# Convolution stage: the moving averages and some low halves go from VectorE to GpSimd, and VectorE's convolution taps move up

## The reference, cut to what matters

```python
def window_mean_minus_self(u, w):        # u: (1, 512, 128) of one group, w in (2, 4, 8, 16)
    cs = cumsum(u, axis=1)
    cs_lag = pad(cs, w)[:, :512]
    cnt = minimum(arange(512) + 1, w)
    return (cs - cs_lag) / cnt - u

def pool_conv_mixer(h, w_in, pool_w, pool_scale, dw_w, dw_b, ln_g, ln_b, w_out):
    u, glu_a, glu_b = split(h @ w_in, [512, 1024])
    pooled = stack([window_mean_minus_self(u[:, :, i], w) for i, w in enumerate((2, 4, 8, 16))])
    ya = einsum("btgc,gcd->btgd", pooled, pool_w) * pool_scale
    gl = glu_a * sigmoid(glu_b)
    cv = causal_dwconv(gl, dw_w) + dw_b      # 31 taps, 512 channels
    yb = silu(layernorm(cv, ln_g, ln_b))
    return concatenate([ya, yb]) @ w_out

# later, in each of two layers: cross attention to 256 memory rows, k, v = split(rmsnorm(mem) @ wkv, 2)
```

## Time and profile before

| What | us |
|---|---|
| Three timed runs | 1711.53, 1709.86, 1711.26; median 1711.26 |
| Profiled execution, first to last instruction (its span; no other time of it is given) | 1710.9 |
| TensorE busy in it | 1684.1 (98%) |
| VectorE busy in it | 1064.3 (62%) |
| GpSimd busy in it | 23.8 (1%) |

### The profile page before, as it was taken

One profiled execution on the slowest core, in us unless ns is written; L12 is line 12 of the kernel. 1 busy time (PEld: TensorE's weight loads), 2 busy tenths in 40 slices (PEclk: granted clock), 3 DMA queues, 4 the chain that ended last, 5 costly groups with the idle time before them and its releaser, 6 DMA issues.

```text
span 1710.9 us, 21153 instructions
## 1 busy us (share of the span) xinstructions
PE 1684.1 (98%) x8045; PEld 1374.0 (80%) x8045; DVE 1064.3 (62%) x1513; ACT 706.7 (41%) x1138; POOL 23.8 (1%) x42
## 2 busy tenths in 40 slices
PE   8999999999999999999999999999999999999998
PEld 7888888788888888887668878888888888977776
DVE  5799763475555532478875446555555767357695
ACT  7313543443333322345764264333332113166674
POOL 1000000000000000011100000000000000000000
PEclk9999999999999999999999999999999999999999
DMA  6272522132222232311104203222227641320201
GB/s 208 82 233 79 170 83 68 50 98 90 91 92 95 98 111 93 91 62 42 50 1 148 99 25 98 98 92 92 92 94 243 202 144 57 116 80 25 75 26 49
DMA packets 154295, 164.40 MB, mean 96 GB/s; under 512 B 2999, under 2 KB 150384, under 8 KB 153968
## 3 DMA queue, kind: packets, MB, share of 16 engines
q1 hardware_dynamic: 153408, 162.51, 29.3%
q0 software_dynamic: 336, 0.53, 0.2%
q10 hardware_dynamic: 479, 0.39, 0.1%
HBM read 160.01 MB, written 3.15 MB: 95 GB/s over the span
## 4 chain that ended last, share of the span: by engine, by line
PE 89%; DVE 6%; ACT 3%; issue 1%; DMA 1%; SPq 0%; DVEq 0%; ACTq 0%
PE bank L928 88%; ACT xa_p L1655 1%; DVE w_lo L2159 1%; PE bank L1354 1%; DMA x_nat<-in_x_dram 1%; DVE nmax L2668 0%; DVE h_lo L2159 0%; ACT w_hi L1655 0%; DVE mla_pT_b L2680 0%; ACT mla_p L1655 0%; DVE xa_pT_lo L2159 0%; DVE fb L2748 0%; PE bank L1614 0%; DVE h_lo L2754 0%; DVE mla_q L2629 0%
## 5 line engine op out<-in xcount | busy, mean ns | idle before, releaser
L928 PE MATMUL bank<-h_hi,w_hi 128*128 128x512 f32 x1472 | 578.9, 393 | 3.1 <-DVE w_lo L2159 1.7
L928 PE MATMUL bank<-h_hi,w_lo 128*128 128x512 f32 x1472 | 573.6, 390 | 0.0
L928 PE MATMUL bank<-h_lo,w_hi 128*128 128x512 f32 x1472 | 573.3, 389 | 0.0
L2159 DVE TENSOR_TENSOR w_lo<-w_raw,w_hi 128x2048 fp32r<-128x2048 f32 (+4 forms) x142 | 286.1, 2019 | 232.1 <-ACT w_hi L1655 231.7
L1655 ACT ACTIVATE w_hi<-w_raw 128x2048 fp32r<-128x2048 f32 (+4 forms) x142 | 239.2, 1690 | 393.6 <-PE bank L928 388.1
L928 PEld LDWEIGHTS bank<-h_hi,w_hi 128*128 128x128 f32 x1472 | 276.2, 188 | 67.8 <-issue 7.1
L928 PEld LDWEIGHTS bank<-h_hi,w_lo 128*128 128x128 f32 x1472 | 276.1, 188 | 58.2
L928 PEld LDWEIGHTS bank<-h_lo,w_hi 128*128 128x128 f32 x1472 | 276.3, 188 | 57.9 <-issue 1.2
L928 PE MATMUL bank<-g_hi,w_hi 128*128 128x512 f32 x352 | 137.6, 391 | 0.0
L928 PE MATMUL bank<-g_hi,w_lo 128*128 128x512 f32 x352 | 137.1, 389 | 0.0
L928 PE MATMUL bank<-g_lo,w_hi 128*128 128x512 f32 x352 | 137.0, 389 | 0.0
(11 more groups left out here) (374 smaller groups left out, 2052.3 us busy)
## 6 DMA issues: line engine op xcount, KB each, us to landing
w_raw<-in_ffn_w_up_dram SPq DMA_DIRECT2D x44, 1024.0 KB, 5.1
w_raw<-in_ffn_w_down_dram SPq DMA_DIRECT2D x16, 1024.0 KB, 5.1
w_raw<-in_w_in_dram SPq DMA_DIRECT2D x13, 1024.0 KB, 5.3
w_whole<-in_xa_wkv_dram SPq DMA_DIRECT2D x12, 1024.0 KB, 5.4
ada_w<-in_w_ada_dram SPq DMA_DIRECT2D x12, 1024.0 KB, 7.8
w_raw<-in_xa_wq_dram SPq DMA_DIRECT2D x8, 1024.0 KB, 5.1
w_raw<-in_xa_wo_dram SPq DMA_DIRECT2D x8, 1024.0 KB, 5.1
w_raw<-in_pc_w_in_dram SPq DMA_DIRECT2D x6, 1024.0 KB, 5.3
```

The costliest lines, as they stand in the source:

```text
L928: return nc.tensor.matmul(o, w, v, start=start, stop=stop, **kw)
L2159: return tt(lo_, v, hi.bitcast(f32), SUB)
```

## The change

GpSimd takes over from VectorE: the low halves of `pc_in` slabs 3, 4 and 5 (`slab_low`), the four moving averages (each a chain of shifted adds in two buffers, two small corrections at the row's start, one scaling by 1/w, one subtraction of the input), the four low halves of the averages (`pooled_low`), and the eight low halves `m1_lo`. VectorE has instead more taps early: 11, 10, 11 and 11 in the steps 2 to 5 (before 8, 7, 8, 8), and then 56 in one go where 80 alternated with the averages; 6 and 19 are left for after `pooled_out((0, 1))` (before 6 and 7). Pairs of semaphores are merged into one with higher counts; that adds and removes no instruction.

```diff
+            def slab_low(n):
+                k = pair_of(n)
+                pool.wait_ge(hi_done, splits_before(n) + 1)
+                pool.wait_ge(lo_done, splits_before(n))
+                nc.gpsimd.tensor_tensor(w_lo[k][:, :], raw[k][:, :], w_hi[k][:, :].bitcast(f32), SUB).then_inc(lo_done, 1)
+
+            slab_low(FIRST["pc_in"] + 3)
             pool.wait_ge(pre_ready, 4 + 2 * DT)
             nc.gpsimd.memset(u_pad[:, :, 0:16], 0.0).then_inc(pads_ready, 1)
+            slab_low(FIRST["pc_in"] + 4)
+            slab_low(FIRST["pc_in"] + 5)
+
+            def pooled_low(g):
+                pool.wait_ge(poolhi_done, g + 1)
+                nc.gpsimd.tensor_tensor(pooled_lo[:, g, :], pooled[:, :], pooled_hi[:, g, :].bitcast(f32), SUB)\
+                    .then_inc(poollo_done, 1)
+
+            pool.wait_ge(pads_ready, 2)
+            pool.wait_ge(consts_done, 1)
+            for g, w in enumerate(WINDOWS):
+                pool.wait_ge(tile_free, TILE0["pc_in"] + 8 + g + 1)
+                src, n, bufs = u_pad[:, g, :], 1, [pool_a, pool_b]
+                wait(pool, pooled_ready, g)
+                while n < w:
+                    dst = bufs[0]
+                    link(nc.gpsimd.tensor_tensor(dst[:, 2 * n - 1:], src[:, 2 * n - 1:], src[:, n - 1:16 + T - n], ADD))
+                    src, n = dst, 2 * n
+                    bufs.reverse()
+                first = src[:, 16:16 + w]
+                link(nc.gpsimd.tensor_scalar(first, first, float(w), None, MUL))
+                link(nc.gpsimd.tensor_tensor(first, first, inv16[:, 0:w], MUL))
+                mean = bufs[0][:, 16:]
+                link(nc.gpsimd.tensor_scalar(mean, src[:, 16:], 1.0 / w, None, MUL))
+                if g:
+                    pooled_low(g - 1)
+                    pool.wait_ge(poollo_done, g)
+                nc.gpsimd.tensor_tensor(pooled[:, :], mean, u_pad[:, g, 16:], SUB).then_inc(pooled_ready, 1)
+            pooled_low(3)
+
+            for i in range(DT):
+                pool.wait_ge(m1_done, DT + i + 1)
+                nc.gpsimd.tensor_tensor(m1_lo[:, i, :], m1[:, i, :], m1_hi[:, i, :].bitcast(f32), SUB).then_inc(mem_lo, 1)
...
-                elif s > 1:
-                    split(n + 1)
...
-                conv([0, 0, 8, 7, 8, 8][s])
-
-            dve.wait_ge(pads_ready, 2)
+                conv([0, 0, 11, 10, 11, 11][s])
+
             dve.wait_ge(tile_free, T0 + 12)
-            dve.wait_ge(consts_done, 1)
-            for s in range(8):
-                g = s // 2
-                if s % 2 == 0:
-                    window(g)
-                else:
-                    dve.wait_ge(poolhi_done, g + 1)
-                    low(pooled_lo[:, g, :], pooled[:, :], pooled_hi[:, g, :]).then_inc(poollo_done, 1)
-                conv(10)
+            conv(56)
...
             pooled_out((0, 1))
             dve.wait_ge(cv_ready, 2)
+            dve.wait_ge(pooled_ready, 4)
             tt(pool_a[:, 0:T], cv[:, 0, :], cv[:, 1, :], ADD).then_inc(ln_added, 1)
             conv(6)
-            for i in range(DT):
-                dve.wait_ge(m1_done, DT + i + 1)
-                low(m1_lo[:, i, :], m1[:, i, :], m1_hi[:, i, :]).then_inc(mem_lo, 1)
+            dve.wait_ge(lo_done, splits_before(AT["kv1", 4]))
             split(AT["kv1", 4])
             conv(len(todo))
```

More of the change, by code:

```diff
@@ L401, in build @@
         mixg_loaded = sem("mixg_loaded")
-        mixg_ready = sem("mixg_ready")
-        mixg_done = sem("mixg_done")
+        mixg_step = sem("mixg_step")
         first_hi = sem("first_hi")
@@ L429, in build @@
         poollo_done = sem("poollo_done")
-        pwhi_done = sem("pwhi_done")
-        pwlo_done = sem("pwlo_done")
+        pw_split = sem("pw_split")
         pool_out = sem("pool_out")
@@ L1644, in _ @@
                 if t == 0:
-                    pe.wait_ge(fsum_ready, 1)
+                    pe.wait_ge(f_sums, 3)
                     for b in range(NB):
@@ L1649, in _ @@
                 if t == 2:
-                    pe.wait_ge(col_sqrt, 1)
+                    pe.wait_ge(col_step, 1)
         @block.scalar
@@ L1763, in _ @@
             a(first[1][:, :, P:], first[0][:, :, P:], ACT.Copy).then_inc(hi_done, 1)
-            act.wait_ge(mixg_done, 1)
+            act.wait_ge(mixg_step, 2)
             first_tiles()
@@ L1866, in cross @@
                         if layer:
-                            act.wait_ge(v1_loaded, 16)
+                            act.wait_ge(v1_moved, 32)
                         else:
@@ L1907, in cross @@
                 if layer == 0:
-                    act.wait_ge(v1_stored, 16)
+                    act.wait_ge(v1_moved, 16)
                 def up_step(it, first=False):
@@ L2033, in _ @@
             cross(1)
-            act.wait_ge(v_ready, 1)
+            act.wait_ge(f_step, 1)
             a(r_col, v_col, ACT.Sqrt).then_inc(f_step, 1)
@@ L2138, in _ @@
             act.wait_ge(stat2_done, 4)
-            a(kv_col[:, :], bank[7][:, 0:NB], ACT.Sqrt, scale=1.0 / D, bias=eps[:, :]).then_inc(col_sqrt, 1)
-            act.wait_ge(col_ready, 1)
+            a(kv_col[:, :], bank[7][:, 0:NB], ACT.Sqrt, scale=1.0 / D, bias=eps[:, :]).then_inc(col_step, 1)
+            act.wait_ge(col_step, 2)
             for t in range(NB):
@@ L2210, in gain_low @@
                     stt(lo_[:, i, :], src(i), param(g, o + i), hi[:, i, :].bitcast(f32), MUL, SUB).then_inc(split_lo, 1)
[L2212 to L2223, removed]
             def pre_copy(r):
@@ L2235, in pre_copy @@
                     cp(memn[:, r - 4 - DT, :], b[:, 0:MEM]).then_inc(pre_done, 1)
-            dve.wait_ge(mixg_ready, 1)
-            cp(prm[:, 0, 0:16], bank[0][:, 0:16]).then_inc(mixg_done, 1)
+            dve.wait_ge(mixg_step, 1)
+            cp(prm[:, 0, 0:16], bank[0][:, 0:16]).then_inc(mixg_step, 1)
             dve.wait_ge(first_hi, 1)
@@ L2296, in _ @@
                 if s == 5:
-                    dve.wait_ge(pwhi_done, 1)
-                    low(pw_lo[:, :, :], pw_raw[:, :, :], pw_hi[:, :, :]).then_inc(pwlo_done, 1)
+                    dve.wait_ge(pw_split, 1)
+                    low(pw_lo[:, :, :], pw_raw[:, :, :], pw_hi[:, :, :]).then_inc(pw_split, 1)
                 for j in range(2):
@@ L2361, in _ @@
             split(AT["kv1", 7])
-            dve.wait_ge(ln_sqrt, 1)
+            dve.wait_ge(ln_summed, 3)
             link(nc.vector.reciprocal(rstd[:, :], rstd[:, :]))
@@ L2740, in _ @@
             link(ts(t_col, f_sum, EPS / D, EPS * EPS, MUL, ADD))
-            stt(v_col, f_weighted, 1.0 / D, t_col, MUL, ADD).then_inc(v_ready, 1)
-            dve.wait_ge(f_step, 1)
+            stt(v_col, f_weighted, 1.0 / D, t_col, MUL, ADD).then_inc(f_step, 1)
+            dve.wait_ge(f_step, 2)
             nc.vector.reciprocal(r_col, r_col).then_inc(root_ready, 1)
@@ L2755, in _ @@
                         ADD, SUB).then_inc(split_lo, 1)
-            dve.wait_ge(f_step, 2)
+            dve.wait_ge(f_step, 3)
             nc.vector.reciprocal(f_col, f_col).then_inc(root_ready, 1)
@@ L2935, in _ @@
             last_square(DT - 1)
-            dve.wait_ge(col_sqrt, 1)
-            nc.vector.reciprocal(kv_col[:, :], kv_col[:, :]).then_inc(col_ready, 1)
-            dve.wait_ge(col_ready, 1)
+            dve.wait_ge(col_step, 1)
+            nc.vector.reciprocal(kv_col[:, :], kv_col[:, :]).then_inc(col_step, 1)
+            dve.wait_ge(col_step, 2)
             for t in range(NB):
```

25 lines of the change are left out of this document (10 added, 15 removed).

## The result

| | before | after |
|---|---|---|
| Runs, median (range), us | 1710.86 (1709.86 to 1711.53), 4 runs | 1718.91 (1718.14 to 1723.48), 4 runs |
| Ratio, 95% interval | | 1.0049 [1.0036, 1.0062] |
| Span of the profiled execution, us | 1710.9 | 1721.8 |

The change makes the kernel 0.49% slower, some 8 us. The execution that was profiled is the slowest of its four; the other spans were 1717.7, 1716.7 and 1716.4.

A forecast was written before the change was run, and what follows sets the result against it. TensorE, busy 98% of the span, was taken to bound the kernel. Slab 4's 5.05, the clock's 1.7 and the tail's 0.7 sum to 7.45 us on 1710.9: 1718.4, plus 0.36 for the median, 1718.7 us (range 1716.0 to 1722.8).

The forecast's parts named there:

- Slab 3 is covered: At slab 3, GpSimd's low half ends about 47.7, 1.4 us before TensorE needs it at 49.05.
- Slab 4, +5.05: At slab 4, TensorE waits for the low half queued behind GpSimd's memset of `u_pad`: +5.05 us, bounds 4.8 and 5.6.
- The clock, +1.7: Behind the idle time at slab 4, TensorE's granted clock falls to half: +1.7 us, bounds 0 and 3.4.
- the clock stays up: Rival, 15%: no half clock behind slab 4's wait, so 5.05 + 0.7 = 5.75 us, 1717.0.
- The tail, +0.7: After `pooled_out`, VectorE's low half of (kv1, 5) comes 0.7 us late for TensorE; `tiles_sum` isn't held.
- The sum: Whole kernel: 5.05 + 1.7 + 0.7 = 7.45 us on the span of 1710.9, giving 1718.4, as median 1718.7.
- It is just in time: VectorE, losing 19.8 us to contention in its taps, reaches `pooled_out` at 153.3, before ScalarE's `y_hi` at 153.9.
- VectorE idle for many microseconds before `pooled_out`: Named sign of being wrong, before `pooled_out`: it would mean contention was charged too dear.
- GpSimd's small instructions: In the averages on GpSimd: 0.2 us for each small instruction, 0.61 us for a scaling.
- ScalarE's waits for the averages are met early: GpSimd starts the averages near 80, some 10 us before VectorE's first one, so ScalarE's waits are met early.
- Contention decides: Rival, 16%: GpSimd blocks VectorE fully, 27 us instead of 20; `pooled_out` 6.7 us late, `tiles_sum` waits: about 1725.

The follow-up runs named there:

- the run with slab 4 alone: The kernel before, with only slab 4's low half moved to GpSimd, behind the memset of `u_pad`: 1720.64 us, ratio 1.0043.
- the run with the busy wait: The changed kernel, with 18 TensorE products ahead of slab 4 into the bank that slab 4 then clears: 1717.63 us, ratio 1.0030.
- without slab 4's stall: The changed kernel, with slab 4's low half moved ahead of GpSimd's wait for the turned memory: 1713.87 us, ratio 1.0015.
- Two buffers: The kernel before, with fourteen unneeded GpSimd products beside the taps, each reading two different buffers: 1724.91 us beside 1710.65 of before.
- the product of 23.03 us: Slab 4's low half first, plus one unneeded GpSimd product after the 11th evacuation, before the third low half: 1714.84 us beside 1710.65 of before.

## Why the prediction was right

It said 1718.7 us (range 1716.0 to 1722.8, slower with 0.93), and 1718.91 came. By its steps, in the profiled execution:

- *Slab 3 is covered*: right. Its low half ended at 47.41, 1.3 us before slab 3 began.
- *Slab 4, +5.05*: right, 4.98. GpSimd's low half took 4.51 us (slab 3's 4.60), against 4.55 from the 128 and 256 column rows. The Trainium skill's 4497 ns (GPSIMD Engine Reference, section 3.1) agrees with the trace's 4.51 to 0.02 us.
- *The clock, +1.7*: mis-sized. The cost was (71.4 - 65.48) / 2 = 3.0 us, near the upper bound of 3.4. I took the spell of the earlier trace rows, behind 2.5 us of idle time; behind 4.7 us it lasted 6.8 us, twice as long, of which 0.9 fell into the wait and cost nothing. In the run with slab 4 alone it cost 2.1, in the run with the busy wait nothing, and there the stage was 2.67 us shorter. The rival "the clock stays up" put its sum at 5.75; the busy wait, which makes it true, had 6.13.
- *The tail, +0.7*: right, 0.88 us of waiting at (kv1, 5), and `tiles_sum` wasn't held.
- *The sum*: 4.98 + 2.96 + 0.88 = 8.82 against the measured 8.80, where I had 7.45. That the median is met to 0.2 us is thus partly luck: a clock term that is 1.3 us too small, against a median of executions that were shorter than the profiled one. How long half clock lasted at slab 4 in those isn't known.
- *"It is just in time"*: this step failed. VectorE's taps ended at 147.19 us, not 153.3, and VectorE stood idle for 6.74. The taps of 80 to 123 us lost 13.95 us (11 in 10.65 and 30 in 30.48 us, at 0.663 unhindered) to 15 products and four scalings, for which I charged 15 x 1.02 + 4 x 0.36 = 16.7. By the single taps six products cost 1.0 us each, eight 0.8, the first nothing, and a scaling the 0.36 that I charged. The other three products that I charged, 3.1 us, cost nothing: one was starved, and the two behind it ran when VectorE had stopped. The sum was spared, as `pooled_out` waited for ScalarE's `y_hi` until 153.92 (predicted 153.9). That this time was met is luck: I took the end of both of ScalarE's instructions, VectorE starts after the first, 0.7 us sooner, and ScalarE was by then 7.4 us late, not 6.75. VectorE idle for many microseconds before `pooled_out` was one of the signs of being wrong that I had named, and it came.
- *GpSimd's small instructions*: mis-priced. A correction took 0.55 us, not 0.2, and the scaling 1.84 to 1.88, not 0.61. They delayed the averages, which had room.
- *ScalarE's waits for the averages are met early*: wrong for the fourth. It waited 3.71 us, hidden here only because TensorE was late; without slab 4's stall 7.64 us, which were on the path.
- *Contention decides*: not here. Two buffers cost 1.02 us a product, as charged, but in the changed kernel VectorE was at `pooled_out` 6.74 us early. And the rival's place was not the first one: `mix_pooled` waits before `tiles_sum` does.

## What to carry to other kernels

Before an instruction moves to a slower engine's queue, look at what stands ahead of it there: one wait that belonged to another job cost 5 us of idle time and 2 to 3 us of clock, and moving one line ahead of it gave back two thirds of the loss. Work that is handed to GpSimd to spare VectorE isn't free while VectorE runs two-input instructions: here each 512-column product took up to 1.02 us from VectorE, more than the 0.66 that VectorE would have spent on it. Between dependent steps on other engines, don't let VectorE run a long unbroken block of such instructions: a GpSimd step that arrives late may have to wait for the end of the block, and whoever needs it waits too.

## What the runs showed of the hardware

- GpSimd and VectorE take turns only if GpSimd comes before VectorE's taps have run long without a break. After the taps had run unhindered for 3.4 us or less it got in at once or after one tap; after 4.4 us or more it stayed out until VectorE paused, ended the block or ran a one-input instruction, for up to 23.03 us. One-input instructions that pass while GpSimd isn't there don't start the count again: the product of 23.03 us came 1.1 us after two of them (one case). Why the length of the run matters is open. The Trainium skill (SBUF — State Buffer, section "Who interferes with whom") says that the two engines contend and that issue order decides who blocks. Here more than that order decides: the product of 23.03 us was there from 121.80 us, and VectorE's taps that began after it went ahead of it.
- The other way round, one VectorE instruction waits for a whole GpSimd one: the product `sq` at 61.47 began 0.55 us behind a low half of 4.51 us and ended 0.55 us behind it, after 4.51 instead of 0.68 us.
- The granted clock fell for 6.8 us around a wait of 4.7 (about 64.6 to 71.4; work resumed at 65.48), and 18 products in that wait kept it at 1.00.
